# Decoder layers with two attention parts on one core: the first eight projections ahead of the last norm, the loop rotated, and two steps of the attention stage moved

## The reference, cut to what matters

```python
def token_mixer(x, ...):
    (ua, ug, q, kc, vc, ks, vs, kw, vw, g_nsa, g_a, g_b) = jnp.split(x @ w_in, cuts, axis=-1)
    u = ua * jax.nn.sigmoid(ug)
    # causal depthwise convolution of u over 31 steps (CONV_W), then a norm, silu and a product
    conv_out = jax.nn.silu(layer_norm(conv, conv_ln_g, conv_ln_b)) @ w_conv_out
    # attention: compressed, selected and window rows, gated by sigmoid(g_nsa)
    attn_out = o.reshape(b, t, N_HEADS * HEAD_DIM) @ w_attn_out
    mixed = jax.nn.sigmoid(g_a) * conv_out + jax.nn.sigmoid(g_b) * attn_out
    return mixed @ w_o, new_state

def decoder_layer(x, start, past, mix, ffn):
    y, state = token_mixer(x, start, past, *mix)
    x = layer_norm(ALPHA * x + y, ln1_g, ln1_b)
    h = jax.nn.silu(x @ w_gate) * (x @ w_up)
    x = layer_norm(ALPHA * x + h @ w_down, ln2_g, ln2_b)
    return x, state
```

## Time and profile before

| | before |
|---|---|
| median of 3 timed runs | 1015.76 us (1015.63 to 1015.79) |
| profiled execution, its own time | 1016.88 us |
| its span | 1015.1 us |
| instructions | 23330 |
| TensorE matmuls, busy | 976.8 us (96%) |
| GpSimd, busy | 748.8 us (74%) |
| VectorE, busy | 600.7 us (59%) |
| ScalarE, busy | 525.6 us (52%) |
| mean granted TensorE clock | 0.993 of 2.4 GHz |

### The profile page before, as it was taken

One profiled execution on the slowest core, in us unless ns is written; L12 is line 12 of the kernel. 1 busy time (PEld: TensorE's weight loads), 2 busy tenths in 40 slices (PEclk: granted clock), 3 DMA queues, 4 the chain that ended last, 5 costly groups with the idle time before them and its releaser, 6 DMA issues.

```text
span 1015.1 us, 23330 instructions
## 1 busy us (share of the span) xinstructions
PE 976.8 (96%) x7438; PEld 927.3 (91%) x7438; DVE 600.7 (59%) x1376; ACT 525.6 (52%) x974; POOL 748.8 (74%) x1081
## 2 busy tenths in 40 slices
PE   6999999989999999999999999999899999999996
PEld 6998879868999999999999977998799999999996
DVE  2969765476686555512457895845776765554125
ACT  4352575555656655533454336664556655555345
POOL 7778746525978888898867785644278888888985
PEclk9999999999999999999999999999899999999999
DMA  8985686722556754455457566676134455555543
GB/s 290 304 265 192 193 280 215 266 63 84 175 161 206 249 189 163 158 179 167 132 188 234 168 188 203 232 237 221 43 104 157 147 160 164 165 167 167 170 142 109
DMA packets 78917, 185.09 MB, mean 182 GB/s; under 512 B 9538, under 2 KB 42690, under 8 KB 78530
## 3 DMA queue, kind: packets, MB, share of 16 engines
q1 hardware_dynamic: 70288, 167.03, 50.3%
q10 hardware_dynamic: 8354, 15.59, 4.6%
q0 software_dynamic: 144, 0.89, 0.2%
HBM read 170.90 MB, written 12.57 MB: 181 GB/s over the span
## 4 chain that ended last, share of the span: by engine, by line
POOL 51%; PE 23%; issue 23%; POOLq 1%; ACT 1%; DVE 1%; DMA 1%; ACTq 0%; SPq 0%; DVEq 0%
POOL w_lo L621 45%; PE proj L693 5%; PE proj L695 5%; PE proj L694 5%; POOL hid L645 3%; POOL res L643 3%; PE proj L716 2%; PE proj L714 2%; PE proj L715 2%; DMA res<-xT_in 1%; POOLq L640 0%; POOLq L615 0%; POOL res L652 0%; ACT x_hi L1103 0%; DVE res L1598 0%
## 5 line engine op out<-in xcount | busy, mean ns | idle before, releaser
L621 POOL TENSOR_TENSOR w_lo<-wch,w_hi 128x256 fp32r<-128x256 f32 x940 | 681.6, 760 | 249.2 <-ACT w_hi L1112 249.0
L693 PE MATMUL proj<-x_hi,w_hi 128*128 128x290 f32 (+1 forms) x1248 | 378.4, 303 | 13.9 <-POOL w_lo L621 11.7
L695 PE MATMUL proj<-x_lo,w_hi 128*128 128x290 f32 (+1 forms) x1248 | 371.1, 297 | 0.0
L694 PE MATMUL proj<-x_hi,w_lo 128*128 128x290 f32 (+1 forms) x1248 | 370.0, 296 | 0.0
L1112 ACT ACTIVATE w_hi<-wch 128x1024 fp32r<-128x1024 f32 x235 | 248.0, 1055 | 139.2 <-PE proj L716 80.8
L693 PEld LDWEIGHTS proj<-x_hi,w_hi 128*128 128x128 f32 x1248 | 236.1, 189 | 17.6 <-DVE x_lo L1512 9.8
L694 PEld LDWEIGHTS proj<-x_hi,w_lo 128*128 128x128 f32 x1248 | 236.5, 190 | 0.6
L695 PEld LDWEIGHTS proj<-x_lo,w_hi 128*128 128x128 f32 x1248 | 236.0, 189 | 0.0
L714 PE MATMUL proj<-hid_hi,w_hi 128*128 128x288 f32 x352 | 104.3, 296 | 0.0
L716 PE MATMUL proj<-hid_lo,w_hi 128*128 128x288 f32 x352 | 104.1, 296 | 0.0
L715 PE MATMUL proj<-hid_hi,w_lo 128*128 128x288 f32 x352 | 103.5, 294 | 0.0
(11 more groups left out here) (292 smaller groups left out, 1532.9 us busy)
## 6 DMA issues: line engine op xcount, KB each, us to landing
wch<-weights_in SPq DMA_DIRECT2D x235, 512.0 KB, 3.7
pg<-slc_pages_in SPq DMA_DIRECT2D x128, 128.0 KB, 2.4
pg<-cmp_pages_in SPq DMA_DIRECT2D x96, 128.0 KB, 3.0
wn<-win_in SPq DMA_DIRECT2D x16, 512.0 KB, 5.0
win_out<-wn ACTq DMA_DIRECT2D x4, 2048.0 KB, 8.4
pg<-cmp_pages_in ACTq DMA_DIRECT2D x32, 128.0 KB, 4.1
hid<-w_in SPq DMA_DIRECT2D x2, 1024.0 KB, 5.8
kv_out<-kv ACTq DMA_DIRECT2D x2, 864.0 KB, 3.5
```

Of the source, the lines that this page charges most:

```text
L621: last = nc.gpsimd.tensor_tensor(lo[:, cols], raw[:, cols], hi[:, cols].bitcast(F32), ALU.subtract)
L693: mm(ps, hi[:, kb], x[0][:, kb, 0:n], start=kb == 0, stop=False)
L694: mm(ps, lo[:, kb], x[0][:, kb, 0:n], start=False, stop=False)
L695: last = mm(ps, hi[:, kb], x[1][:, kb, 0:n], start=False, stop=kb == KD - 1)
```

## The change

It has three parts.

The first eight projections ahead of the last norm. They now work as gate and up do: on the shifted blocks times `g2`, in tensors of their own (`xr_hi`, `xr_lo`) that lie in places of the attention and of the hidden values, with two further columns for -g2 and b2. ScalarE rounds these blocks during the down product (`features_raw`), VectorE makes their low parts (`low_raw`). The loop is rotated: the end of a layer holds only the statistics, the deviation and its reciprocal; centering, scaling, `g2` and `b2`, and the rounding to `x_hi` and `x_lo` stand at the head of the next layer, between the corrections of projections 0 to 7, and after the loop for the output. Layer 0 runs the same code with mean 0, deviation 1, `g2` 1 and `b2` 0. The fillers are gone. `g2` and `b2` are kept in `gb2`, so that the small tensor of the next layer is loaded earlier. The page loads on ScalarE's queue, one with each of projections 2 to 17 before, stand now two with each of 6 to 9 and one with each of 10 to 17. All 44 taps that stood between and behind `take_u(2)` and `take_u(3)` stand behind them.

The group's rows. VectorE's `group_copy` and `group_out` of the second group stand ahead of `unit_first(5)`.

The read. ScalarE's `fill_out` that stood behind the exponentials of the first group and the copy of `conv_hi` stands ahead of these exponentials.

```diff
-STEADY = {"norm": 29, "block": 2}
+RAW = 2 * KC
+ACT_PAGES = {o: 2 if o < 10 else 1 for o in range(6, EARLY)}
```

SyncE's queue:

```diff
-                    if j == (SLOTS - 1 if first else SLOTS + 1):
-                        wait_alone(*x_ready(layer, 0))
+                    if j == (SLOTS - 1 if first else 0):
+                        wait_alone(*sm_free(layer, 0))
```

GpSimd: `center_half` has a further wait, and its taps wait for `u_taken(KC)` and `x_lo_ready(KD)`:

```diff
+                    pool.wait_ge(*raw_lo_ready(layer, KD))
```

TensorE, `project_x`:

```diff
-                n = TOKX if O_GU <= o < O_DOWN else TOK
+                n = TOKX if O_GU <= o < O_DOWN or o < RAW else TOK
...
+                    if o == 0:
+                        pe.wait_ge(*raw_lo_ready(layer, kb + 1 - KD))
...
+                    x_h, x_l = (xr_hi[:, kb], xr_lo(kb)) if o < RAW else (x[0][:, kb], x[1][:, kb])
...
-                    if first == -KD and kb < KD - 1:
-                        for _ in range(STEADY["block"]):
-                            mm(ps_m[:, 0:TOK], hi[:, kb], x_hi[:, kb, 0:TOK], start=True, stop=True)
...
-                keep_busy(STEADY["norm"])
```

ScalarE, head of a layer and the read behind the first group's exponentials:

```diff
-                for n in range(KC):
-                    if n >= 2:
-                        act.wait_ge(*out_read[1](layer, n - 1))
-                    read_out(2 * n, sig_u[:, n % 2], ACT.Tanh, scale=0.5)
-                    chunk_read(2 * n)
-                    chunk_read(2 * n + 1)
+                act.wait_ge(*rstd_ready(layer, 0))
+                do(rstd_sb, rstd_ps, ACT.Copy, rstd_copied, wait=False)
+                act.wait_ge(*out_done(layer, 1))
+                chunk_read(0)
+                affine(layer, 0)
+                gate(0)
+                features_rounded(layer, 0)
+                act.wait_ge(*out_done(layer, 2))
+                chunk_read(1)
+                affine(layer, 1)
+                features_rounded(layer, 1)
+                chunk_read(2)
+                affine(layer, 2)
+                gate(1)
+                features_rounded(layer, 2)
+                chunk_read(3)
+                affine(layer, 3)
+                features_rounded(layer, 3)
+                chunk_read(4)
+                gate(2)
+                chunk_read(5)
+                chunk_read(6)
+                gate(3)
+                chunk_read(7)
...
                 window_out(0)
+                fill_out()
                 group_act(layer, 0, 1)
                 act.wait_ge(*conv_act(layer, 1))
                 do(conv_hi[:].rearrange("p k t -> p (k t)"), sq[:, 0:KC * TOK], ACT.Copy, conv_hi_ready)
-                fill_out()
```

ScalarE in the down stage, `features_raw` behind each square, and the old end of a layer:

```diff
+                                    for pair in range(2):
+                                        features_square(layer, 1, pair)
+                                        features_raw(layer, 2 * pair)
+                                        features_raw(layer, 2 * pair + 1)
...
-                        for c in range(KD):
-                            if c % 2 == 0:
-                                act.wait_ge(*normed(layer, 7 + c // 2))
-                            do(resv[:, c], resv[:, c], ACT.Identity, x_ready, scale=gn[:, c:c + 1], bias=bn[:, c:c + 1], wait=False)
-                            if c:
-                                act.wait_ge(*x_ready(layer, KD + c))
-                                do(x_hi[:, c - 1, 0:TOK], resv[:, c - 1], ACT.Copy, x_hi_ready, wait=False)
```

VectorE, head of a layer, and the attention stage:

```diff
+                def unshift_raw(o, sums_at):
+                    dve.wait_ge(*out_done(layer, o + 1))
+                    do(v.tensor_copy(sums_at, bank[o % 2][:, TOK:TOKX]))
+                    read_out(o, v.scalar_tensor_tensor(out=fixed_ps, in0=mean_sb, scalar=sums_at[:, 0:1], in1=bank[o % 2][:, 0:TOK],
+                                                       op0=ALU.mult, op1=ALU.add))
+                def fix_gate(c):
+                    unshift_raw(2 * c, sums_of[:, 0])
+                    do(v.tensor_scalar(sums_of[:, 2, c % 2:c % 2 + 1], sums_of[:, 0, 1:2], 0.5, None, ALU.mult), wait=False)
+                    do(v.tensor_tensor(gate_ps, fixed_ps, rstd_sb, ALU.mult), gate_fixed)
...
+                dve.wait_ge(*raw_lo_ready(layer, 0))
+                norm_pair(layer, 0)
+                fix_gate(0)
+                norm_pair(layer, 1)
                 take_u(0)
+                norm_pair(layer, 2)
+                fix_gate(1)
+                norm_pair(layer, 3)
                 take_u(1)
+                for c in range(4):
+                    low_features(c)
+                fix_gate(2)
+                for c in range(4, KD):
+                    low_features(c)
+                take_u(2)
...
+                fix_gate(3)
+                take_u(3)
...
-                convolve(8)
-                take_u(2)
-                convolve(10)
-                take_u(3)
-                convolve(26)
+                convolve(44)
...
                 fill_out()
-                unit_first(layer, 5)
                 group_copy(layer, 1)
                 group_out(layer, 1)
+                unit_first(layer, 5)
```

VectorE, end of a layer and after the loop:

```diff
-                features_in(layer, 1, lambda c: None)
-                features_norm(layer, low_features)
+                features_in(layer, 1, low_raw)
+                take_variance(layer, 1, sd)
+                dve.wait_ge(*sd_ready(layer, 3))
+                do(v.reciprocal(rstd_ps, sd), rstd_ready)
...
+            for pair in range(KD // 2):
+                norm_pair(DEPTH, pair, copied=False)
```

More of the change, by code:

```diff
@@ L948, in _ @@
                 state["out"] = 0
[L950 to L951 removed]
+                for o in range(RAW):
+                    project_x(layer, o, o, None)
                 pe.wait_ge(*nsa_ready(layer, 1))
@@ L2022, in _ @@
                 sig.end()
+            now["layer"] = DEPTH
+            dve_order.count = normed.count = 0
+            for pair in range(KD // 2):
+                norm_pair(DEPTH, pair, copied=False)
 def _arrange(a):
```

176 lines of the change are left out of this document (114 added, 62 removed).

## The result

The changed kernel took 1017.72 us in the median of 20 runs (1014.53 to 1020.77), the kernel before 1015.88 us (1013.88 to 1019.68) in as many: a ratio of 1.0017 with a 95% interval of 1.0009 to 1.0025. I had forecast 1013.5 us, faster; it is 1.8 us slower.

The account below looks back on a forecast made before the run. TensorE, busy for 96% of the span, was taken to set the pace, with GpSimd close behind. Terms -5.5 + 2.6 + 0 - 2.4 - 1.8 + 3.4 + 0.6 + 0.4 + 0.4 summed to -2.3 us: 1013.5 us, range 1007 to 1018.5.

Parts of the forecast that it names:

- The seam: Between the layers: projections start before the norm is done, VectorE's read then sets projection 7's start; -5.5 us.
- rival (a): At seam and ropes: VectorE keeps up, low parts at 0.46 us, no lateness; about 1006.9 us; 13%.
- (d): At the seam: the jump costs TensorE more than VectorE, so projections do not come forward; 1016.5 us; 5%.
- The tail: Last norm after the loop: no rounding between its affines, so the last block is ready sooner; -2.4 us.
- The five roundings in the down stage: ScalarE, between two weight chunks in the down stage: five roundings of 0.43 us; +0.4 us, from 0 to 1.
- What VectorE hands on: From gates to compression: VectorE's late taps and ropes pass 1.3 us to TensorE; +2.6 us for two layers.
- The start: Head of layer 0: fillers dropped, but VectorE holds projections 6 and 7 about as much; 0, from -1.4 to +1.
- The read: Attention stage: ScalarE's read fits its idle 1.26 us, exponentials move by 0.4 at most; -1.8 us for two layers.
- The group's rows: Attention stage: the wait before the group's transpose goes, but unit 5's maxima chain starts later; +3.4 us for two layers.
- the clock: Attention stage, layer 0: half of layer 1's 1.2 us loss at the lower clock, added for the longer stall; +0.6 us.
- Rival (b): Attention stage: the rows' copy ahead costs nothing, as something else already holds the maxima chain; 1009.5 us; 20%.
- rival (c): Gates to ropes: VectorE becomes the bound, its list to the first tap costing 2 us more; 1019.5 us; 22%.

Follow-up runs that it names:

- e13: e10 with eight taps before the compression's first step on VectorE, and two of the four inside it, moved behind that step: ratio 0.9949 to the kernel before.
- e8: e2 with 12 of the 44 first taps of the convolution left out, so not the whole computation: ratio 0.9952 to the kernel before.
- e1: The changed kernel run again unaltered: ratio 1.0017 to the kernel before.
- e3: The changed kernel with ScalarE's read put back behind the first group's exponentials and the copy of conv_hi: ratio 1.0021 to the kernel before.
- e4: The changed kernel with both the group's rows and the read put back, leaving the rotated loop alone: ratio 0.9959 to the kernel before.
- the square of runs: e1, e2, e3 and e4 on one chip, with the rows and the read each ahead or put back: ratios 1.0017, 0.9956, 1.0021, 0.9959.
- e12: The changed kernel with 15 calls, 30 small unread matmuls, in the wait before the values of unit 4: ratio 0.9996 to the kernel before.
- e2: The changed kernel with the group's rows put back behind the maxima of unit 5: ratio 0.9956 to the kernel before.
- e5: The kernel before with only the group's rows moved ahead of the maxima of unit 5: ratio 1.0048 to the kernel before.
- e10: e4 with VectorE's maxima of unit 5 and the copy of the rows ahead of unit 4's weights: ratio 0.9935 to the kernel before.
- e11: The kernel before with VectorE's maxima of unit 5 and the copy of the rows ahead of unit 4's weights: ratio 0.9962 to the kernel before.
- e6: The changed kernel with ScalarE's copies of unit 4's transposed weights ahead of unit 5's exponentials: ratio 1.0040 to the kernel before.
- e9: The changed kernel with 30 calls, each two small unread matmuls, in the wait before the values of unit 4: ratio 1.0016 to the kernel before.

## Why the prediction was wrong

**The seam (-5.5) was right.** From the end of the statistics to the gates -4.95 us, 0.2 us of the difference being the two columns. I had VectorE's read of projection 5 end 28.6 us behind the statistics (528.5 - 499.9); it ended at 532.4, 28.5 us behind them. TensorE's jump cost 3.94 us of idle time (I took 3.5), VectorE's 3.39 (I took 4.1), a low part of the first four 0.89 us (I took 0.85). What differed was small: the second four took 1.57 us, and the visible wait fell on projection 6 (0.80 us) alone. So rival (a) with low parts at 0.46 us is refuted (the median is 0.98; its seam should also have been 518.1 - 509.7 = 8.4, not 8.1), and so is (d): the jump took 0.4 us more than I had, not 3. The Trainium skill ("Runtime: NRT & Kernel Launch", Instruction fetch mechanics) has a taken branch cost a fetch when its target isn't among the pages at hand, and both waits for issue agree. The Trainium skill's rule that a VectorE instruction with two SBUF inputs and a GpSimd one that reads SBUF exclude each other ("SBUF — State Buffer", Who interferes with whom) would allow 1.2 us for a low part, by my estimate; the changed kernel's sixteen stayed below 1.0 us (a single line: count, ns min/median/max, first and last start us):

```profile
L1884 DVE TENSOR_TENSOR x_lo<-res,x_hi x16: 453/983/998, 27.8 to 531.3; 128x288 fp32r<-128x288 f32 x16
```

**The tail (-2.4) was right:** -2.5 us. The five roundings in the down stage (+0.4) cost nothing that the traces show: 265.27 against 265.45 us, and 264.75 against 265.42.

**What VectorE hands on (+1.3 a layer) was a little low:** +1.8 us a layer at the compression, and at 15 of the 19 waits of 2.6 us a clock at 1.2 GHz for 3.4 to 6.8 us. The place was right, the sum had a slip: the first rope 562.9 - 557.46 = 5.4 us late, less 0.56 + 2.24 + 0.81 = 3.6 us of idle time, is 1.8, not 1.3. That this hits the measured 1.8 is luck: against the gates the first rope came only 4.1 us late, the idle time went as reckoned, and the four ropes took 6.9 us in sum where they had taken 5.4. e13's way of moving it only moved the wait, and in e8 taking it away gave 0.4 us, which is nothing that its interval can tell.

**The start (0, to +1) was low by 1 to 2.5 us in most traces.** The eleven profiles of the rotated loop in which the low parts stand as the change has them show 39.4 to 42.0 us to the first gates, the three of the old loop 39.4, 39.4 and 40.8. The blocks of four low parts took 2.66 and 3.73 us in the first trace of the changed kernel, 3.7 and 3.7 in e1, e3 and e4; the waits at projections 6 and 7 go with them, 1.5 us in the first trace and 2.7 in e1.

These four make my -4.5 (with +0.4 for the columns and +0.4 for the roundings, and without the two small parts); e4 measured -4.2, between -2.5 and -5.9. That the two lie so close is in part luck: outside the attention stage e4's trace is 3.2 us shorter than that of before; the rest of its gain lies in that stage, where before's layer 1 took 102.00 us.

**The read (-1.8) was wrong.** The step that failed is "these move by 0.4 at most". ScalarE had 1.26 us of idle time ahead of the exponentials, but the issue of the window rows' store (`window_out`) lay in it, which does not count as busy. In every trace with the read ahead the issue starts 0.23 us behind the work before it, and the read begins 0.73 to 0.77 us behind that work; only the last 0.5 us was free, for a read and a chunk that hold ScalarE for 1.26 us:

```profile
143.94 1.16 ACT L1134 ACTIVATE sq<-hid 128x1152 f32<-128x1152 f32 x1
145.33 0.40 ACTq L1422 DMA_DIRECT2D win_out<-wn  x1
145.83 0.41 ACT L1142 ACTIVATE hid<-proj 128x288 f32<-128x288 f32 x1 [0.74 <-ACT sq L1134]
147.09 1.17 ACT L1134 ACTIVATE res<-res,top 128x1056 f32<-128x1056 f32 x1
...
154.00 0.40 ACT L1134 ACTIVATE res<-res,unit_top 128x128 f32<-128x128 f32 x1 [2.25 <-DVE unit_top L1756]
```

Layer 0 stood 1.86 us later here than before (the group's scores at 135.80 against 133.94), so 147.09 is 0.7 us later than 144.51 would be. VectorE's normalising, the maxima of unit 0 and its exponentials follow (154.00, against 150.75 before, 1.4 us later by the same measure), and so does ScalarE's copy of the group's transposed weights, for which the scores of unit 1 wait: 1.12 us where there had been no wait. The gain was given back within 10 us; by the square of runs the read is worth 0.4 us or -0.3, not 1.8.

**The group's rows (+3.4, and +0.6 for the clock) had the right mechanism and a size too small.** The forecast's signs hold one by one: the maxima behind the copies out, a wait of 3.81 us (I had 3.7), the chain 1.8 to 2 us later in each layer (3.8 us by e12, I had 3.4). The whole, 4.0, measured 6.2 and 6.3 us (give or take 2) and 4.9 (give or take 1.4). The term that was mis-sized is the clock, as far as is known: I took half of 1.2 us; by e12 it came to about 2.1, give or take 1.9, by the traces to 0.8 and 1.1 behind these waits. That the rows ahead keep the clock down more is plain from all executions: its mean is 0.984 in the changed kernel and in e1 and 0.982 in e3, against 0.989 in e4 and in e12. How the rest of the 6 us splits stays open.

In the profile of before the clock had fallen in one layer of two behind 2.32 us of waiting; behind 3.81 us it fell in both layers of all four traces with the rows ahead (first trace, e1, e3, e5), for 6.8 us except once 3.4. One trace of before was no measure of how often it falls, or of what the stage takes without a fall. Rival (b), that the copy is free, is refuted by e2, e4 and e5, and rival (c), that VectorE's lateness alone makes the kernel slower, by e4.

So: -4.2 for the rotated loop, 0 for the read, +6 for the rows make +1.8 us, against -4.5 - 1.8 + 4.0 = -2.3. Of the 4.1 us between, the read is 1.8, the rows are 2, the rotated loop 0.3.

Open also stays how much of the lateness at the compression reaches the end in layer 1, and why the start of layer 0 varies by 1.4 us in the old loop too.

## What to carry to other kernels

A wait of the busiest engine is not worth its length: ask which chain ends it, and move work only where the chain's next step starts sooner (e10, e11), not where the engine merely stands (the rows, e6, e13). Before using another engine's idle time, look at what lies in it: here the issue of a store, which no busy share shows, took 0.7 of 1.26 us. And take more than one trace before pricing a clock, or trusting a difference of 0.2%: here the profiled execution was the fastest of twenty and pointed the wrong way, and the one that I summed against was 1 us slower than its kernel's median.

## What the runs showed of the hardware

The jump at the end of the loop's body left TensorE idle for 3.55 to 4.05 us in the twelve traces of the rotated loop, where its next work lies ready, and VectorE for 3.4 to 4.7 us. With the fillers ahead of the jump only 1.90 us stood idle on TensorE.

Which stalls lower the clock is not a matter of their length alone: behind the same 2.33 us it was at 1.2 GHz for 3.4 us (e4) or 6.8 us (e2, layer 0), or not at all (before, layer 0); behind 3.81 us always; behind waits of 0.95 and 0.75 us not (e10), but behind the same wait of 1.3 us in layer 1 (at 649.48 in e3) it fell for 3.4 us in e3, e10 and e11 and not in e4 and e5. What a fall costs grows faster than its length: from the compression to the first group's scores, with the wait of 2.6 us ahead, it took 46.1 to 46.3 us with 6.8 us at 1.2 GHz (5 cases), 44.8 to 45.5 with 3.4 us (10), and 44.8 to 44.9 with none (4).

Matmuls that nobody reads, put into a stall and no longer than it, kept the clock up and were worth 2.1 us in 1016, give or take 1.9 (e12); twice as many were worth nothing (e9).
